# Streaming both activation halves behind one weight load in the last two layers of a two-block model

## The reference, cut to what matters

```python
u = h @ w_in
q, k, v, g_ret, z, xbc, dt, gate_ret, gate_ssd = jnp.split(u, ...)
...
yr = (jax.nn.silu(g_ret) * normed(retention(q, k, v)))      # 2048 wide
o_ret = yr @ ret_out                                        # 2048 -> 1024
...
ys = ssd_scan(...) + d_skip * xs
ys = ys * jax.nn.silu(z)                                    # z: 2048 wide
ys = normed(ys) * ssd_norm_w
o_ssd = ys @ ssd_out                                        # 2048 -> 1024
merged = jax.nn.sigmoid(gate_ret) * o_ret + jax.nn.sigmoid(gate_ssd) * o_ssd
return merged @ w_o
```

## Time and profile before

| | us |
|---|---|
| runs shown | 2480.3, 2478.26, 2480.83 (median 2480.3) |
| the profiled execution | 2481.6 |
| its span | 2479.8 |
| PE busy | 2313.0 (93%), 18844 matmuls |
| PE weight loads busy | 2241.0 (90%) |
| VectorE busy | 1689.8 (68%) |
| ScalarE busy | 1247.5 (50%) |

### The profile page before, as it was taken

How to read it: one execution, slowest core, us unless ns; L and a number is a source line. 1 busy time by engine, 2 the same in 40 slices (tenths; PEclk the granted TensorE clock), 3 DMA queues, 4 the chain that set the end, 5 groups by cost and what they waited for, 6 DMA issues and landing times.

```text
span 2479.8 us, 50538 instructions
## 1 busy us (share of the span) xinstructions
PE 2313.0 (93%) x18844; PEld 2241.0 (90%) x18844; DVE 1689.8 (68%) x2602; ACT 1247.5 (50%) x1744; POOL 0.3 (0%) x5
## 2 busy tenths in 40 slices
PE   6899799978997999799999999999899999999998
PEld 6788799978887999799989889999899999889998
DVE  6877777558777676476684667775656775576774
ACT  4243366542343665435544763664435536645654
POOL 0000000000000000000000000000000000000000
PEclk9999899988998999999999999999999999999999
DMA  5333455543333455444435335555544354345554
GB/s 183 103 103 111 128 172 184 191 139 123 103 120 114 158 186 187 161 162 162 137 131 175 120 111 187 178 184 189 163 162 153 122 168 140 125 145 170 188 187 160
DMA packets 104266, 377.21 MB, mean 152 GB/s; under 512 B 11408, under 2 KB 13712, under 8 KB 103824
## 3 DMA queue, kind: packets, MB, share of 16 engines
q1 hardware_dynamic: 101888, 368.10, 44.9%
q10 hardware_dynamic: 2192, 6.52, 0.8%
HBM read 373.52 MB, written 1.05 MB: 151 GB/s over the span
## 4 chain that ended last, share of the span: by engine, by line
PE 77%; DVE 13%; issue 6%; ACT 3%; DMA 1%; DVEq 0%; ACTq 0%
PE acc L537 21%; PE acc L538 21%; PE acc L539 21%; DVE w_lo L1303 2%; PE mid L660 2%; PE mid L512 1%; PE acc L607 1%; PE acc L609 1%; PE acc L608 1%; ACT w_hi L998 1%; PE mid L888 1%; PE mid L904 1%; DVE zs L1496 1%; PE mid L917 1%; PE mid L890 1%
## 5 line engine op out<-in xcount | busy, mean ns | idle before, releaser
L1303 DVE TENSOR_TENSOR w_lo<-w_raw,w_hi 128x1024 fp32r<-128x1024 f32 x699 | 853.1, 1223 | 412.7 <-ACT w_hi L998 390.3
L998 ACT CAST w_hi<-w_raw 128x1024 fp32r<-128x1024 f32 x699 | 731.5, 1048 | 517.1 <-PE acc L539 490.9
L537 PE MATMUL acc<-h_hi,w_hi 128*128 128x256 f32 x2240 | 660.2, 295 | 19.7 <-DVE w_lo L1303 10.8
L538 PE MATMUL acc<-h_lo,w_hi 128*128 128x256 f32 x2240 | 642.4, 287 | 0.0
L539 PE MATMUL acc<-h_hi,w_lo 128*128 128x256 f32 x2240 | 641.9, 287 | 0.0
L537 PEld LDWEIGHTS acc<-h_hi,w_hi 128*128 128x128 f32 x2240 | 439.1, 196 | 29.8 <-DVE w_lo L1303 13.8
L538 PEld LDWEIGHTS acc<-h_lo,w_hi 128*128 128x128 f32 x2240 | 439.1, 196 | 0.8
L539 PEld LDWEIGHTS acc<-h_hi,w_lo 128*128 128x128 f32 x2240 | 438.1, 196 | 0.0
L539 PE MATMUL acc<-g_hi,w_lo 128*128 128x256 f32 x1376 | 386.4, 281 | 0.0
L537 PE MATMUL acc<-g_hi,w_hi 128*128 128x256 f32 x1376 | 386.4, 281 | 0.0
L538 PE MATMUL acc<-g_lo,w_hi 128*128 128x256 f32 x1376 | 386.4, 281 | 0.0
(11 more groups left out here) (345 smaller groups left out, 3741.0 us busy)
## 6 DMA issues: line engine op xcount, KB each, us to landing
w_raw<-weights_d SPq DMA_DIRECT2D x700, 512.0 KB, 3.3
p<-p_d ACTq DMA_DIRECT2D x2, 1080.0 KB, 5.2
rdec<-decay_d ACTq DMA_DIRECT2D x2, 768.0 KB, 5.0
x<-x_d ACTq DMA_DIRECT2D x1, 1024.0 KB, 11.4
out_d<-work SPq DMA_DIRECT2D x4, 256.0 KB, 2.2
c<-c_d ACTq DMA_DIRECT2D x1, 712.0 KB, 12.4
p<-p_d ACTq DMA_DIRECT2D x2, 244.0 KB, 2.6
c<-c_d ACTq DMA_DIRECT2D x1, 448.0 KB, 3.2
```

The costliest lines, as they stand in the source:

```text
L537: mm(dst, wh, hi[:, k, :], start=first and j == 0, stop=False)
L538: mm(dst, wh, lo[:, k, :], start=False, stop=False)
L998: nc.scalar.copy(w_hi[:, slot, :], w_raw[:, slot, :]).then_inc(hi_done, 1)
L1303: tt(w_lo[:, slot, :], w_raw[:, slot, :], w_hi[:, slot, :].bitcast(F32), SUB).then_inc(lo_v, 1)
```

## The change

For the slabs 72 to 135 but for none of the others, a matmul streams both halves of the activations behind one load of the high weights: 512 columns, the high half's product in the first 256 columns of the bank, the low half's in the last 256. The low weights' matmul adds into the first 256. Of 24 matmuls a slab keeps 16, eight of them 512 columns wide. To make this one access pattern, `h_hi`/`h_lo`, `r_hi`/`r_lo` and `s_hi`/`s_lo` become halves of one buffer each, at the same addresses as before. The sum of the two halves of the bank is made by VectorE with a `tensor_reduce` over the pair (`halves_sum`). For the gates and `z` it stands in `gate_sum`, and ScalarE then applies its function in place in SBUF (`gate_of`). For the 2048-row products `halves_sum` stands ahead of the multiplication, which now reads SBUF.

```diff
+            def slab_folded(at, i, t):
+                weights_of(at, i)
+                bank(at, t)
+                slot = i % RING
+                both = acc[t % 4][:, :].rearrange("p (a t) -> p a t", a=2)
+                for k in range(KD):
+                    a = slice(k * P, k * P + P)
+                    mm(both, w_hi[:, slot, a], h[:, :, k, :], start=k == 0, stop=False)
+                    done = mm(acc[t % 4][:, 0:T], w_lo[:, slot, a], h_hi[:, k, :], start=False, stop=k == KD - 1)
+                done.then_inc(used, 1)
...
+            def slabs_long_folded(at, i, t, both, need=None):
+                bank(at, t)
+                wide = acc[t % 4][:, :].rearrange("p (a t) -> p a t", a=2)
...
+                        mm(wide, w_hi[:, slot, a], both[:, :, k, :], start=k == 0, stop=False)
+                        done = mm(acc[t % 4][:, 0:T], w_lo[:, slot, a], both[:, 0, k, :], start=False, stop=k == NI - 1)
...
+                elif Z20 <= i < RO_S:
+                    slab_folded(at, i, i)
...
+            def gate_of(at, t, y, func):
+                wait_out(act, at, t)
+                nc.scalar.activation(y, y, func).then_inc(a_gate, 1)
...
                 elif Z20 <= i < RO_S:
                     b = i - Z20
-                    act.wait_ge(v_flo, at.n * 16 + (b + 1))
-                    evac(at, i, i, yr[:, b, :], acc[i % 4][:, 0:T], ACT.Silu)
+                    gate_of(at, i, yr[:, b, :], ACT.Silu)
...
+            def halves_sum(y, t):
+                return nc.vector.tensor_reduce(y, acc[t % 4][:, :].rearrange("p (a t) -> p t a", a=2), AX_X, ADD)
+
+            def gate_sum(at, i, t, y):
+                wait_used(dve, at, i)
+                halves_sum(y, t).then_inc(out[t % 4], 1)
...
+                elif Z20 <= i < RO_S:
+                    gate_sum(at, i, i, yr[:, i - Z20, :])
                 elif RO_S <= i < SO_S:
                     n, part = (i - RO_S) // 3, (i - RO_S) % 3
-                    if part == 2:
+                    if part == 0:
+                        gate_sum(at, i, RO_T + 2 * n, sg[:, n % 2, :])
+                    elif part == 2:
                         t = RO_T + 2 * n + 1
                         wait_used(dve, at, i)
-                        wait_out(dve, at, t - 1)
-                        tt(work[:, n, :], acc[t % 4][:, 0:T], sg[:, n % 2, :], MUL).then_inc(out[t % 4], 1)
+                        gate_ready(at, GATE_RO + n)
+                        halves_sum(work[:, n, :], t).then_inc(out[t % 4], 1)
+                        wait_out(dve, at, t)
+                        tt(work[:, n, :], work[:, n, :], sg[:, n % 2, :], MUL).then_inc(dve_step2, 1)
+                        dve.wait_ge(dve_step2, own.next())
+                elif SO_S <= i < SO_S + KD:
+                    gate_sum(at, i, SO_T + i - SO_S, sgs[:, i - SO_S, :])
```

More of the change, by code:

```diff
@@ L69 @@
 XB = 24
+GATE_Z, GATE_RO, GATE_SO, GATES = 0, NI, NI + KD, NI + 2 * KD
 TRI = 3 * P
@@ L104 @@
 V_STEPS1 = 72
-V_STEPS2 = 150
+V_STEPS2 = 166
 TWO_PI = 6.283185307179586
@@ L227, in hybrid_kernel @@
         x = place("x", [P, KD, T])
[L228 to L229 removed]
+        h = place("h", [P, 2, KD, T], F32R)
+        h_hi, h_lo = h[:, 0, :, :], h[:, 1, :, :]
         work_at = top[0]
@@ L586, in slab_k4 @@
                 done.then_inc(used, 1)
+            def slabs_long_folded(at, i, t, both, need=None):
+                bank(at, t)
+                wide = acc[t % 4][:, :].rearrange("p (a t) -> p a t", a=2)
+                for m in range(2):
+                    weights_of(at, i + m)
+                    slot = (i + m) % RING
+                    for j in range(KD):
+                        k, a = m * KD + j, slice(j * P, j * P + P)
+                        if need is not None:
+                            need(k)
+                        mm(wide, w_hi[:, slot, a], both[:, :, k, :], start=k == 0, stop=False)
+                        done = mm(acc[t % 4][:, 0:T], w_lo[:, slot, a], both[:, 0, k, :], start=False, stop=k == NI - 1)
+                    done.then_inc(used, 1)
             def slabs_long(at, i, t, n, blocks, hi, lo, need=None):
@@ L1227, in second_slab @@
                     b = i - Z20
-                    act.wait_ge(v_flo, at.n * 16 + (b + 1))
-                    evac(at, i, i, yr[:, b, :], acc[i % 4][:, 0:T], ACT.Silu)
+                    gate_of(at, i, yr[:, b, :], ACT.Silu)
                 elif RO_S <= i < SO_S and (i - RO_S) % 3 == 0:
                     n = (i - RO_S) // 3
[L1232 to L1237, removed]
+                    gate_of(at, RO_T + 2 * n, sg[:, n % 2, :], ACT.Sigmoid)
                 elif SO_S <= i < SO_S + KD:
                     n = i - SO_S
-                    evac(at, i, SO_T + n, sgs[:, n, :], acc[(SO_T + n) % 4][:, 0:T], ACT.Sigmoid)
+                    gate_of(at, SO_T + n, sgs[:, n, :], ACT.Sigmoid)
                 elif WO_S < i:
@@ L1870, in second_slab @@
                         wait_used(dve, at, i)
-                        wait_out(dve, at, SO_T + n)
-                        tt(y, acc[t % 4][:, 0:T], sgs[:, n, :], MUL).then_inc(out[t % 4], 1)
+                        gate_ready(at, GATE_SO + n)
+                        halves_sum(y, t).then_inc(out[t % 4], 1)
                         wait_out(dve, at, t)
-                        wait_out(dve, at, RO_T + 2 * n + 1)
+                        tt(y, y, sgs[:, n, :], MUL).then_inc(dve_step2, 1)
+                        dve.wait_ge(dve_step2, own.next())
                         tt(work[:, n, :], work[:, n, :], y, ADD).then_inc(dve_step2, 1)
```

21 lines of the change are left out of this document (12 added, 9 removed).

## The result

The changed kernel takes 2512.78 us (median of 5 runs, 2508.83 to 2516.83), the kernel before 2480.83 in as many. The ratio is 1.0127 [1.0116, 1.0139]: slower by 32 us, where 22 were forecast. The profiled execution took 2510.36 us, its span is 2508.5.

The account below looks back on a forecast made before the run. PE was taken to bound z and slabs 88 to 111, VectorE slabs 112 to 121. Terms summed to 11.0 us a layer, 22.0 in two, on 2481.6; the median 1.3 lower gave 2502 us, range 2484 to 2538, own case 2493 to 2512.

Parts of the forecast that it names:

- the loop: In z, sum, silu, cast and w_lo wait on each other: 3.26 us a turn against PE's 2.75 a slab.
- The sum at 0.68: VectorE's new tensor_reduce over a bank's two halves: 0.68 us each, 48 a layer, bounds 0.42 and 1.21.
- rival 1: Each VectorE sum costs 1.21 us, as pair halves lie 1 KB apart: 19 us a layer, 2540 us; chance 0.10.
- z, +4.4: Slabs 72 to 87: PE gets the first scan step's mt 4.4 us later a layer, PE's savings in z included.
- The low clock, +1.6: Behind PE's 5 us standstill before the first mt product its clock falls: 1.6 us lost a layer.
- Slabs 88 to 111, -0.5: Scan groups: four get 0.13 us longer, three with a norm's mean save 0.31 each; with the ends -0.5 a layer.
- The wide matmul at 224: On PE, a 512-column matmul takes 224 ns to its successor, between 216 and 240.
- Rival 4: On PE, the wide stream gains nothing (240 ns), with the loops as forecast: 2508 us; chance 0.11.
- Slabs 112 to w_o, 5.3: Per layer: roots later +3.2, four sums +2.4, slab 123's cast +0.4, clock at slab 122 +0.5, 13 long slabs -1.2.
- Into w_o, +0.2: The last product's chain into w_o gets one more VectorE operation, mostly hidden: +0.2 us a layer.
- Rival 2: The sum costs 0.42 us or the loop has fewer links; about 3 us a layer left, 2486 us; chance 0.10.
- Rival 3: In the three stages on PE the fold pays and the loops are absorbed: 7.0 us a layer saved, 2466; chance 0.11.

Follow-up runs that it names:

- e2: Changed kernel, but in z ScalarE takes each silu one place later, behind the next cast; fold and sums stay: 2494.80 us, ratio 1.0045.
- e4: Changed kernel with all sums and their order, but z and both gates unfolded to 24 narrow matmuls a slab: 2514.19 us, ratio 1.0126.
- e6: As e2, and ScalarE also takes the other gates' sigmoids later: gate_ret's behind the scan step's sums, gate_ssd's one slab later: 2487.78 us, ratio 1.0026.
- e1: Changed kernel, but the z slabs as before the change: narrow matmuls, silu straight from the bank, no sum: 2497.19 us, ratio 1.0061.
- e8: Changed kernel, but VectorE reads the norm's mean out of mid[3] ahead of the long slab's sum and multiplication: 2506.05 us, ratio 1.0095.
- e3: Changed kernel's folded matmuls without any sums; only the first 256 columns are read, with the waits of before: 2474.29 us, ratio 0.9965.
- e5: Changed kernel, same order and waits, but VectorE copies the bank's first half instead of summing both halves: 2490.20 us, ratio 1.0030.
- e9: e6 and e8 together, with gate_ssd unfolded and its sigmoid straight from the bank, without a sum: 2476.27 us, ratio 0.9976.

## Why the prediction came out as it did

2502 was forecast, 2512.8 measured, in the stated range but just above the case's own (2493 to 2512). The mechanism is the forecast's: e2 and e4 show the loop, e6 the roots. The trace has 15.1 us for layer one up to the feed-forward part, where the steps said 11.0.

- **The sum at 0.68:** measured 0.683. That refutes rival 1: pairs 1 KB apart in PSUM cost VectorE no more than 512 columns in a row. The penalty for jumps between cache lines that the Trainium skill states ("SBUF — State Buffer", Door 1: The DMA port swizzle) doesn't show in this trace for such reads; of PSUM that sentence speaks for matmuls alone.
- **z, +4.4:** measured +4.3 (213.94 - 209.65). The turn was 3.26 in the forecast and 3.25 in the trace. The forecast has `w_lo` waits from slab 85 on; there was one, of 0.23 us, because PE's slab takes 2.85 and not 2.75: the room of 4.4 us, at 3.25 - 2.85 = 0.40 a turn, lasts 11 turns. That changed nothing at the end, since the loop sets it.
- **The low clock, +1.6:** the mis-sized step. The rows of before show two waits of about 2 us, each with some 3.5 us at 1.2 GHz behind it, and I put one such stretch behind a wait of 5 us. There the low stretch is twice as long (a mean of 0.54 over 7.40 us is 6.8 us at half speed; 0.57 over 4.00 is 3.4), and the second `mt` product comes 2.9 late. e1 and e2 give these back: 2.66 and 2.68 of "1 to 16". In layer two the low stretch lasts 10.2 us, part of it within the wait, and costs 3.65 (8.55 us from the first to the second product, before 4.90).
- **Slabs 88 to 111, -0.5:** the step that failed, with its sign. A group without a mean got 0.13 longer, as worked out (12.71 for 12.58). The three with a mean were to win 0.31 each and lost 0.59. I had checked that `mt` is early there and stopped; its product also needs the bank, and the read that frees it is queued behind the sum. e8 takes exactly that away. With the groups as they are the stage costs +2.0 instead of -0.5.
- **The wide matmul at 224:** measured 236 and 230. The value was nearer to the upper bound, "twice 120". The rule of the Trainium skill ("TensorE: Matmul & The Clock Gate", Back-to-back issue gap), given there for an isolated matmul, had 216 for it and nearly nothing gained; the trace has 14 to 20 more for the wide one and 8 to 11 more for the narrow one, so the overhead grows with the width here, and a little is gained. Rival 4 was nearly right on this price (240) and wrong on its effect: in z and in the groups of after PE's saving is hidden by the loops, as e4 shows.
- **Slabs 112 to w_o, 5.3:** measured 5.5, of which the roots +3.3 (forecast 3.2), the four sums +2.3 (2.4), slab 123 4.53 us behind `w_lo` of 122 (4.54). Two errors cancel, which is luck: the clock at slab 122 was full (1.00 from 1510.33 to 1513.58, so 0 for +0.5; in e6 and e8 it was not), and 13 long slabs gave 0.5 instead of 1.2.
- **Into w_o, +0.2:** measured +0.4; without sums it is 25.52 (e3), with the cheap ones 25.68 (e5), with the others 25.8 to 25.95.

Together, in a layer: -0.1 in z, +1.3 of clock, +2.5 of the groups, +0.2 and +0.2 of the last two steps, 4.1 more than the forecast: the 15.1 and 11.0 of above. From there to the last v matmul of layer two it is 0.6 more. The clock is low for 13.6 us of that stretch in after and for 10.2 in before; e2, with after's code there, has 10.3 and is 0.9 shorter than after, so this is not the change's cost. Layer two, to the end, is 15.3 us longer. From the v slabs of layer one to the end after is 31.0 us longer than before; its profiled execution had been 2.4 us ahead up to there, in code that the change doesn't touch.

Rival 2 was run as e5: 2490 for 2486. It had some 3 us a layer left; the stretches of e5 add up to 3.2, and the medians are 9.6 apart. Rival 3, PE's saving with the loops absorbed, was priced at 2466; with the sums gone altogether (e3) it is 2474, and with sums that are kept out of the way (e9) 2476.

## What to carry to other kernels

When an operation is put between two engines that already hand work to each other, add up one turn around both queues, with everything queued between; compare that with the pace of the engine that you want to relieve, not with the busy shares. If the turn is longer, it is often enough to let the next hand-over pass ahead of the new work (e2), and cheapest not to put it into the stretch whose bound is the engine that would do it (e9). And when you say that an operand will be early, check also the bank or buffer that its consumer writes, and what its last reader is queued behind.

## What the runs showed of the hardware

- Two halves streamed behind one load of fp32r weights cost 236 ns (230 in the products) for 512 columns, where two matmuls with a load each cost 240 (234). So a load that is saved is worth 4 ns by these, and 5 to 6 by the triple.
- VectorE's `tensor_reduce` over pairs 1 KB apart in PSUM costs 683 ns for 512 columns, as much as its two-operand instruction over 512 columns; a copy of 256 costs 417 (e5).
- The low clock lasts longer with a wait of 4.5 us (6.8 us in layer one of after, 10.2 in layer two) than behind one of 2.08 (3.4 us). Behind the waits of 0.69 us in three groups a layer the granted clock stayed at 1.00.
- The same wait need not have the same clock behind it: behind PE's 2.89 us ahead of z it was low for 3.4 us in 17 of 20 layers and stayed at 1.00 in three, in executions of different kernels with the same code there. This is worth about 1.5 us, as much as some of the edits.
